# VectorE mixes the older block ahead of the last logits chunk of the newer one, in the second attention stage

## The chip, the cores and the metric

The kernel runs on one core of one Trainium2 chip. The metric is the device time of one execution in microseconds (us), inputs and output in the chip's memory.

## The reference, cut to what matters

The kernel computes a two-layer decoder trunk over 2048 tokens of width 1024. Layer 0 is a sparse attention, layer 1 a differential attention; each has its projections, a gate and an output projection. The change touches layer 1 alone:

```python
    def block(args):                      # one block of 128 queries, 8 heads, 2 maps each
        qb, start = args
        t = start + jnp.arange(BLOCK_Q)
        rel = t[:, None] - key_pos[None, :]
        bias = rel_bias[t5_bucket(rel)].astype(jnp.float32)
        logits = jnp.einsum('bqmd,blmd->bmql', qb, k).astype(jnp.float32)
        logits = logits + jnp.moveaxis(bias, -1, 0)[None]
        logits = jnp.where((rel >= 0)[None, None], logits, -jnp.inf)
        p = jax.nn.softmax(logits, axis=-1).reshape(bsz, B_HEADS, 2, BLOCK_Q, L)
        a = p[:, :, 0] - lam * p[:, :, 1]
        return jnp.einsum('bhql,blhe->bqhe', a.astype(v.dtype), v)
```

So for each head and block of queries there are two softmax maps; the second, scaled, is subtracted from the first, and the difference multiplies the values.

## The kernel before, in words

Both attention stages are written by one function, `stage_attention`; the second one is called with two maps (`M == 2`) and 8 heads. Each engine has its own program, and all of them walk the same list of places: 16 places a head, one block of 128 queries each, in the order of `ORDER` (blocks 2, 3, 6, 7, 10, 11, 14, 15, 12, 13, 8, 9, 4, 5, 0, 1 at places 0 to 15). Block b has (b + 1) x 128 keys, cut into chunks of up to 512, so there are 1, 1, 2, 2, 3, 3, 4, 4, 4, 4, 3, 3, 2, 2, 1, 1 chunks at places 0 to 15. "(p, i)" below is chunk i at place p, always both maps.

- **TensorE** (`logits`, `turn`, `values` in its program). A pair of logits chunks goes to two of four buffers in PSUM (`s_ps`, `SR = 4`), so the pair (p, i) may be written when VectorE has read the pair two before it. At place p TensorE issues (p, 1), (p, 2), (p, 3), each with one quad (up to 4 transposes) of the mixed block of place p - 3 beside it, then (p + 1, 0), then matmuls with the values. The transposes go to two PSUM buffers (`t_ps`, `TR = 2`) that ScalarE empties: the third quad waits for ScalarE's copy of the first.
- **VectorE** (`logits`, `invert`, `maximum`, `mix`). It copies each chunk out of PSUM to SBUF with bias and a running maximum (lines 1255, 1257), combines the maxima (line 1263), inverts the sum of the second map of the block before (line 1267, it waits for both exponentials of that block), makes the factor -lambda l1 / l2 (line 1273), and adds the scaled second map to the first (line 1275, the mix).
- **ScalarE** (`exps`, `leave`, `output`). At place p it computes both exponentials of the block of place p - 1 in place, with their sums (line 1321, waits for the maximum), then copies the transposes of the block of place p - 3 to SBUF (line 1329), then an output block (line 1338).

Each engine executes in its written order. `walk` writes places 0 to 5 of the first head, then a loop whose pass is places 6 to 15 of one head and 0 to 5 of the next, then the rest; so VectorE's loop jumps back between places 5 and 6.

## Time and profile before

| | us |
|---|---|
| median of 3 runs | 3835.47 |
| lowest, highest | 3829.93, 3839.96 |
| the profiled execution | 3832.36 |
| its span | 3830.6 |
| VectorE's part of the second attention stage | about 2784 to 3547 |

The profile shows one execution. "Busy" of an engine counts its instructions; an idle time carries the name of what ended it. TensorE's matmuls (PE) and weight loads (PEld) are counted apart. PEclk is TensorE's granted clock as a share of 2.4 GHz. In a timeline a row can stand for several instructions in a row (x4). Loads and matmuls wait separately, so one wait can be seen twice.

### The profile page before, as it was taken

To read this page: it belongs to the slowest core of one execution; us is meant where nothing else is said; L and a number is where in the kernel's file an instruction comes from. 1 tells how busy PE (TensorE), PEld (TensorE's weight loads), DVE (VectorE), ACT (ScalarE), POOL (GpSimd) and SP (SyncE) were. 2 spreads that over 40 slices of the span, in tenths; PEclk is the share of its full clock that TensorE was granted. 3 is DMA by queue.
4 is the path that set the end of the run, shared out by engine and by line. 5 is a ranking of instruction groups with operands and counts; after the bars stand their busy time and mean duration, and the time that the engine had idled before them with its cause. 6 is when DMAs were issued, how large, how long until landed. Compare 5 with 4: busy or idle time off the path is not lost. (4 is left out here: it accounts for less than half of the span.)

```text
span 3830.6 us, 65352 instructions
## 1 busy us (share of the span) xinstructions
PE 3446.8 (90%) x18786; PEld 2574.8 (67%) x18786; DVE 2133.8 (56%) x5870; ACT 2015.2 (53%) x3490; POOL 523.1 (14%) x550
## 2 busy tenths in 40 slices
PE   5869898888999999998966999999989988989799
PEld 3746454476666666666855888889966666666687
DVE  3659999995555555555643111000087777777343
ACT  3548799946777777774223111111066666666222
POOL 2000255001111111110211111111020000000011
PEclk7989999978999999998987999999989999999798
DMA  9651689573223322324532444222142222221442
GB/s 236 184 135 33 201 236 237 172 228 102 76 79 82 84 75 76 85 73 164 173 138 83 120 121 118 87 71 69 58 130 70 70 70 70 70 70 31 138 143 99
DMA packets 430048, 436.43 MB, mean 114 GB/s; under 512 B 81793, under 2 KB 341281, under 8 KB 429601
## 3 DMA queue, kind: packets, MB, share of 16 engines
q1 hardware_dynamic: 419072, 430.93, 38.6%
q10 hardware_dynamic: 10784, 3.18, 0.9%
q8 instruction: 92, 1.51, 0.2%
q14 instruction: 100, 0.81, 0.1%
HBM read 271.44 MB, written 162.53 MB: 113 GB/s over the span
## 5 line engine op out<-in xcount | busy, mean ns | idle before, releaser
L1255 DVE CUSTOM_DVE_ANT_0 a_att_sb_lg<-a_att_ps_s,mask 128x512 f32<-128x512 f32 (+3 forms) x512 | 302.2, 595 | 217.7 <-PE a_att_ps_s L1147 176.8
L1329 ACT ACTIVATE a_att_sb_pT<-a_att_ps_t 128x512 f32<-128x512 f32 (+3 forms) x640 | 315.9, 530 | 104.9 <-PE a_att_ps_t L1166 98.0
L1321 ACT ACTIVATE b_att_sb_lg<-b_att_sb_lg,b_att_sb_negm 128x384 f32<-128x384 f32 (+15 forms) x256 | 305.6, 1198 | 123.2 <-DVE b_att_sb_negm L1263 123.0
L1153 PE MATMUL b_att_ps_s<-b_att_sb_k,b_att_sb_q 64*128 64x512 f32 (+3 forms) x1920 | 297.1, 420 | 75.2 <-DVE b_att_sb_lg L1257 59.8
L1321 ACT ACTIVATE a_att_sb_lg<-a_att_sb_lg,a_att_sb_negm 128x384 f32<-128x384 f32 (+15 forms) x256 | 307.3, 1201 | 78.3 <-DVE a_att_sb_negm L1263 78.3
L1166 PE MATMUL a_att_ps_t<-ident,a_att_sb_lg 128*128 128x128 f32 x2176 | 340.0, 279 | 0.0
L1257 DVE TENSOR_SCALAR_CACHE_REDUCE b_att_sb_lg<-b_att_ps_s 128x512 f32<-128x512 f32 (+3 forms) x512 | 283.1, 590 | 90.1 <-PE b_att_ps_s L1153 75.0
L1694 DVE TENSOR_SCALAR_CACHE_REDUCE mask<-scores,threshold_bits 128x384 bf16<-128x384 f32 (+8 forms) x288 | 322.6, 1187 | 1.2
L1166 PEld LDWEIGHTS a_att_ps_t<-ident,a_att_sb_lg 128*128 128x128 f32 x2176 | 248.8, 141 | 107.3 <-issue 57.3
L1146 PE MATMUL a_att_ps_s<-a_att_sb_k,a_att_sb_q 128*128 128x512 f32 (+3 forms) x640 | 287.2, 449 | 26.5 <-DVE a_att_sb_mx L1255 15.7
L1183 PE MATMUL a_att_ps_o<-a_att_sb_pT,a_att_sb_v 128*64 128x256 f32 (+1 forms) x2304 | 297.4, 377 | 0.5 <-DMA a_att_sb_v<-scratch_v 0.5
L1664 ACT ACTIVATE mask<-scores,threshold_bits 128x1152 bf16<-128x1152 f32 (+4 forms) x160 | 274.6, 1717 | 22.4 <-DVE threshold_bits L1711 16.2
L1153 PEld LDWEIGHTS b_att_ps_s<-b_att_sb_k,b_att_sb_q 64*128 64x128 f32 x1920 | 164.8, 200 | 158.0 <-DVE b_att_sb_lg L1257 84.8
L1186 PE MATMUL b_att_ps_o<-b_att_sb_pT,b_att_sb_v 128*128 128x256 f32 (+1 forms) x1152 | 270.9, 384 | 0.0
L1610 PE MATMUL select_ps_acc<-select_sb_h,select_sb_w_gate 128*128 128x512 f32 x512 | 237.5, 619 | 29.6 <-DMA select_sb_w_gate<-in_a_w_in 20.7
L1186 PEld LDWEIGHTS b_att_ps_o<-b_att_sb_pT,b_att_sb_v 128*128 128x128 f32 x1152 | 214.7, 194 | 59.9 <-issue 18.2
L1114 POOL TENSOR_TENSOR a_att_sb_near_mask<-a_att_sb_near,mask 128x256 f32<-128x256 f32 x224 | 147.7, 671 | 729.6 <-DVE a_att_sb_mx L1255 377.1
L1329 ACT ACTIVATE b_att_sb_pT<-b_att_ps_t 128x512 f32<-128x512 f32 (+2 forms) x320 | 159.1, 527 | 158.6 <-PE b_att_ps_t L1166 157.7
L1147 PE MATMUL a_att_ps_s<-a_att_sb_k,a_att_sb_q 128*128 128x512 f32 (+3 forms) x640 | 235.2, 367 | 0.0
L1183 PEld LDWEIGHTS a_att_ps_o<-a_att_sb_pT,a_att_sb_v 128*64 128x64 f32 x2304 | 149.0, 136 | 120.9 <-issue 55.6
L405 DVE SCALAR_TENSOR_TENSOR b_qkgv_sb_o_lo<-b_qkgv_ps_acc,b_qkgv_sb_o_hi 128x512 f32<-128x512 f32 x64 | 44.2, 691 | 317.8 <-ACT b_qkgv_sb_o_hi L391 317.8
L391 ACT ACTIVATE b_qkgv_sb_o_hi<-b_qkgv_ps_acc 128x512 fp32r<-128x512 f32 x64 | 38.3, 599 | 324.3 <-PE b_qkgv_ps_acc L376 324.3
(282 smaller groups left out, 6941.7 us busy)
## 6 DMA issues: line engine op xcount, KB each, us to landing
a_att_sb_q<-scratch_qT SPq DMA_DIRECT2D x512, 64.0 KB, 2.6
select_sb_w_gate<-in_a_w_in SPq DMA_DIRECT2D x32, 512.0 KB, 5.6
mask_sb_mod_w<-in_mod_w SPq DMA_DIRECT2D x16, 1024.0 KB, 6.6
a_att_sb_k<-scratch_kT SPq DMA_DIRECT2D x128, 128.0 KB, 2.9
b_qkgv_sb_w<-in_b_w_in SPq DMA_DIRECT2D x32, 512.0 KB, 4.9
b_att_sb_q<-scratch_qT SPq DMA_DIRECT2D x128, 128.0 KB, 2.5
b_att_sb_k<-scratch_kT SPq DMA_DIRECT2D x64, 256.0 KB, 4.1
front_sb_mod_w<-in_mod_w SPq DMA_DIRECT2D x8, 1024.0 KB, 6.4
```

What stands on the lines that cost most here:

```text
L1146: nc.tensor.matmul(out, q[:, p // 2 % QS, 0, cols], k[:, slot, a:z], start=True, stop=False)
L1153: mm = nc.tensor.matmul(s_ps[:, (n + m) % SR, 0:z - a], q[rows, p // 2 % QS, x, cols], k[rows, slot, y, a:z], start=(j == 0), stop=(j == 2))
L1166: x = nc.tensor.transpose(t_ps[:, n % TR, j - a], lg[:, p % LR, j * P:(j + 1) * P], ident[:])
L1183: x = nc.tensor.matmul(o_ps[half, r % 2, a:PAIR], v[:, slot, j], pT[:, r % 2, j, a:PAIR], start=(j < 2 and not j == last == 1), stop=(j >= ...
L1186: x = nc.tensor.matmul(o_ps[:, r % 2, a:PAIR], v[:, slot, j], pT[:, r % 2, j, a:PAIR], start=(j == 0), stop=(j == last))
L1255: x = nc.vector.tensor_tensor_reduce(out, src, tab, 1.0, 2 * NEG, sign, ALU.max, top[:, col:col + 1])
L1257: x = nc.vector.tensor_scalar(out, src, 1.0, 2 * NEG, ALU.mult, ALU.max, accum_out=top[:, col:col + 1])
L1321: nc.scalar.activation(buf, buf, ACT.Exp, bias=negm[:, p, m:m + 1], accum_out=sums[:, b, ds(h * M + m, 1)]).then_inc(exp_done, 1)
L1329: nc.scalar.activation(pT[:, r % 2, a:z, c:c + P], t_ps[:, n % TR, 0:z - a], ACT.Copy).then_inc(t_left, 1)
L1610: m = nc.tensor.matmul(acc[:, t % RA], w_gate[:, j % 2, k], h[:, k], start=(k == 0), stop=(k == KD - 1))
L1664: nc.scalar.activation(junk[:, o:o + N], scores[:, o:o + N], ACT.Sign, bias=bits[:, place:place + 1].bitcast(F32), accum_out=cnt[:, place: ...
L1694: nc.vector.tensor_scalar(junk[:, o:o + N], scores[:, o:o + N], bits[:, place:place + 1].bitcast(F32), 0.0, ALU.is_ge, ALU.add, accum_out= ...
```

## The change

In VectorE's program `invert` and `mix` of the older block (place p - 1) are called together, ahead of the last chunk pair of the newer block (place p), and the maximum of the newer block comes behind that pair. Before, `invert` came behind the last chunk pair, then the maximum, and `mix` last. No instruction is added or taken away, and the programs of the other engines and the first attention stage (`M == 1`) stay as they are.

```diff
+            def mixing(h, p, before):
+                if M == 2:
+                    for head, x in both(h, p, before):
+                        if 1 <= x <= NB:
+                            invert(head, x - 1)
+                            mix(head, x - 1)
+
...
             def place(h, p, before):
                 if h is not None:
                     for i in range(NCH[p]):
+                        if i == NCH[p] - 1:
+                            mixing(h, p, before)
                         for m in range(M):
                             logits(h, p, i, m)
-                if M == 2:
-                    for head, x in both(h, p, before):
-                        if 1 <= x <= NB:
-                            invert(head, x - 1)
-                if h is not None:
                     maximum(h, p)
+                else:
+                    mixing(h, p, before)
                 for head, x in both(h, p, before):
                     for r in outputs_here(x):
                         output(head, r)
-                    if M == 2 and 1 <= x <= NB:
-                        mix(head, x - 1)
```

On VectorE, place 6 (block 14, four chunks) of the last head, before. `b_att_sb_lg` are the logits in SBUF, `b_att_ps_s` those in PSUM, `b_att_sb_mx` the maxima of the chunks, `b_att_sb_negm` the negated maximum; the mix of 1536 columns is that of block 11:

```order
L1257 TENSOR_SCALAR b_att_sb_lg,b_att_sb_mx<-b_att_ps_s 128x512 x6
L1257 TENSOR_SCALAR b_att_sb_lg,b_att_sb_mx<-b_att_ps_s 128x128
L1255 ISA b_att_sb_lg,b_att_sb_mx<-b_att_ps_s,b_att_sb_near 128x256
L1255 ISA b_att_sb_mx 128x1
L1257 TENSOR_SCALAR b_att_sb_lg,b_att_sb_mx<-b_att_ps_s 128x128
L1255 ISA b_att_sb_lg,b_att_sb_mx<-b_att_ps_s,b_att_sb_near 128x256
L1255 ISA b_att_sb_mx 128x1
L1267 RECIPROCAL b_att_sb_rec<-sums 128x1
L1263 TENSOR_REDUCE b_att_sb_negm<-b_att_sb_mx 128x2
L1273 SCALAR_TENSOR_TENSOR b_att_sb_ratio<-sums,b_att_sb_rec,neglam 128x1
L1275 SCALAR_TENSOR_TENSOR b_att_sb_lg<-b_att_sb_lg,b_att_sb_ratio 128x1536
```

And now:

```order
L1257 TENSOR_SCALAR b_att_sb_lg,b_att_sb_mx<-b_att_ps_s 128x512 x6
L1267 RECIPROCAL b_att_sb_rec<-sums 128x1
L1273 SCALAR_TENSOR_TENSOR b_att_sb_ratio<-sums,b_att_sb_rec,neglam 128x1
L1275 SCALAR_TENSOR_TENSOR b_att_sb_lg<-b_att_sb_lg,b_att_sb_ratio 128x1536
L1257 TENSOR_SCALAR b_att_sb_lg,b_att_sb_mx<-b_att_ps_s 128x128
L1255 ISA b_att_sb_lg,b_att_sb_mx<-b_att_ps_s,b_att_sb_near 128x256
L1255 ISA b_att_sb_mx 128x1
L1257 TENSOR_SCALAR b_att_sb_lg,b_att_sb_mx<-b_att_ps_s 128x128
L1255 ISA b_att_sb_lg,b_att_sb_mx<-b_att_ps_s,b_att_sb_near 128x256
L1255 ISA b_att_sb_mx 128x1
L1263 TENSOR_REDUCE b_att_sb_negm<-b_att_sb_mx 128x2
```

The inversion, the factor and the mix of block 11 moved from behind the last chunk pair of block 14 (two pieces of 128 and 256 columns a map) to ahead of it, and the maximum of block 14 closes the place.

On VectorE, the end of the loop's pass (place 5, block 11), before:

```order
L1261 REGISTER_ALU
L1262 REGISTER_ALU
L1263 TENSOR_REDUCE b_att_sb_negm<-b_att_sb_mx 128x2
L1272 REGISTER_ALU
L1273 ISA
L1273 SCALAR_TENSOR_TENSOR b_att_sb_ratio<-sums,b_att_sb_rec,neglam 128x1
L1274 REGISTER_ALU
L1275 SCALAR_TENSOR_TENSOR b_att_sb_lg<-b_att_sb_lg,b_att_sb_ratio 128x1408
L992 REGISTER_ALU
L992 COMPARE_AND_BRANCH
```

And now:

```order
L1257 TENSOR_SCALAR b_att_sb_lg,b_att_sb_mx<-b_att_ps_s 128x256
L1255 ISA b_att_sb_lg,b_att_sb_mx<-b_att_ps_s,b_att_sb_near 128x256
L1255 ISA b_att_sb_mx 128x1
L1239 REGISTER_ALU
L1257 TENSOR_SCALAR b_att_sb_lg,b_att_sb_mx<-b_att_ps_s 128x256
L1255 ISA b_att_sb_lg,b_att_sb_mx<-b_att_ps_s,b_att_sb_near 128x256
L1255 ISA b_att_sb_mx 128x1
L1261 REGISTER_ALU
L1262 REGISTER_ALU
L1263 TENSOR_REDUCE b_att_sb_negm<-b_att_sb_mx 128x2
L992 REGISTER_ALU
L992 COMPARE_AND_BRANCH
```

The mix of block 10 (1408 columns) was the last operation ahead of the jump; now the last chunk pair of block 11 and its maximum are.

## Rows read from the trace of the kernel before

**Rows 1.** The page, part 1: busy time, share of the span and instructions.
```profile
PE 3446.8 (90%) x18786; PEld 2574.8 (67%) x18786; DVE 2133.8 (56%) x5870; ACT 2015.2 (53%) x3490; POOL 523.1 (14%) x550
```

**Rows 2.** Busy time in eight stretches, one for each head of the stage: the sum.
```profile
sum 746.00, PE 670.64 PEld 478.80 DVE 591.61 ACT 474.98 POOL 20.26; mean PE 83.83 PEld 59.85 DVE 73.95 ACT 59.37 POOL 2.53
```

**Rows 3.** Waits, 2700 to 3600 us: engine line <- releaser, total us, times, longest.
```profile
ACT b_att_sb_lg L1321 <- DVE b_att_sb_negm L1263: 123.0, 65, 7.4
...
DVE b_att_sb_lg L1257 <- PE b_att_ps_s L1153: 75.0, 48, 7.3
...
PE b_att_ps_s L1153 <- DVE b_att_sb_lg L1257: 59.8, 57, 5.8
...
DVE b_att_sb_rec L1267 <- ACT b_att_sb_lg L1321: 9.7, 9, 3.9
...
PE b_att_ps_t L1166 <- DVE b_att_sb_lg L1275: 6.7, 2, 3.6
```

**Rows 4.** VectorE in time, blocks 6 and 7: start us, us, engine, line, operation, [idle <-releaser].
```profile
3077.03 0.29 DVE L1257 TENSOR_SCALAR_CACHE_REDUCE b_att_sb_lg<-b_att_ps_s 128x128 f32<-128x128 f32 x1 [1.55 <-PE b_att_ps_s L1153]
...
3078.35 0.17 DVE L1263 TENSOR_REDUCE b_att_sb_negm<-b_att_sb_mx 128x2 f32<-128x16 f32 x1
...
3078.82 0.75 DVE L1275 SCALAR_TENSOR_TENSOR b_att_sb_lg<-b_att_sb_lg,b_att_sb_ratio 128x512 f32<-128x512 f32 x1
...
3079.49 0.68 DVE L1257 TENSOR_SCALAR_CACHE_REDUCE b_att_sb_lg<-b_att_ps_s 128x512 f32<-128x512 f32 x1
...
3080.71 0.42 DVE L1257 TENSOR_SCALAR_CACHE_REDUCE b_att_sb_lg<-b_att_ps_s 128x256 f32<-128x256 f32 x1
```

**Rows 5.** ScalarE in time, the two exponentials of block 6.
```profile
3078.65 1.05 ACT L1321 ACTIVATE b_att_sb_lg<-b_att_sb_lg,b_att_sb_negm 128x896 f32<-128x896 f32 x1 [1.95 <-DVE b_att_sb_negm L1263]
...
3080.62 0.19 ACT L1321 ACTIVATION_READ_ACCUMULATOR b_att_sb_lg<-b_att_sb_lg,b_att_sb_negm  x1
```

**Rows 6.** VectorE in time: end and start of a loop pass, and other such starts.
```profile
3093.75 1.69 DVE L1275 SCALAR_TENSOR_TENSOR b_att_sb_lg<-b_att_sb_lg,b_att_sb_ratio 128x1408 f32<-128x1408 f32 x1
...
3098.15 0.69 DVE L1257 TENSOR_SCALAR_CACHE_REDUCE b_att_sb_lg<-b_att_ps_s 128x512 f32<-128x512 f32 x1 [2.72 <-issue]
...
3387.11 0.69 DVE L1257 TENSOR_SCALAR_CACHE_REDUCE b_att_sb_lg<-b_att_ps_s 128x512 f32<-128x512 f32 x1 [3.83 <-issue]
```

**Rows 7.** VectorE in time, the maximum of block 14 and, a place later, its mix.
```profile
3008.60 0.17 DVE L1263 TENSOR_REDUCE b_att_sb_negm<-b_att_sb_mx 128x2 f32<-128x16 f32 x1
...
3016.85 2.22 DVE L1275 SCALAR_TENSOR_TENSOR b_att_sb_lg<-b_att_sb_lg,b_att_sb_ratio 128x1920 f32<-128x1920 f32 x1
```

**Rows 8.** ScalarE in time, block 14: two exponentials, then copies of transposes.
```profile
3008.89 1.90 ACT L1321 ACTIVATE b_att_sb_lg<-b_att_sb_lg,b_att_sb_negm 128x1920 f32<-128x1920 f32 x1 [3.65 <-DVE b_att_sb_negm L1263]
...
3012.58 0.18 ACT L1321 ACTIVATION_READ_ACCUMULATOR b_att_sb_lg<-b_att_sb_lg,b_att_sb_negm  x1
...
3012.67 1.06 ACT L1329 ACTIVATE b_att_sb_pT<-b_att_ps_t 128x512 f32<-128x512 f32 x2
```

**Rows 9.** TensorE in time, places 7 to 10.
```profile
3013.80 2.03 PE L1153 MATMUL b_att_ps_s<-b_att_sb_k,b_att_sb_q 64*128 64x512 f32 x12
...
3015.76 1.99 PE L1186 MATMUL b_att_ps_o<-b_att_sb_pT,b_att_sb_v 128*128 128x256 f32 x8
...
3018.12 0.96 PE L1153 MATMUL b_att_ps_s<-b_att_sb_k,b_att_sb_q 64*128 64x512 f32 x6
...
3036.27 0.96 PE L1153 MATMUL b_att_ps_s<-b_att_sb_k,b_att_sb_q 64*128 64x512 f32 x6
```

**Rows 10.** TensorE in time, place 6 of the next head.
```profile
3102.56 1.65 PE L1153 MATMUL b_att_ps_s<-b_att_sb_k,b_att_sb_q 64*128 64x512 f32 x6 [0.44 <-DVE b_att_sb_lg L1257]
...
3104.14 3.35 PE L1186 MATMUL b_att_ps_o<-b_att_sb_pT,b_att_sb_v 128*128 128x256 f32 x8
```

**Rows 11.** Stretches: us, busy of PE, PEld, DVE, ACT, POOL, then granted clock.
```profile
3099.50:3107.50 8.00, 7.55 (x27) 5.37 (x28) 7.10 (x24) 3.45 (x3) 0.00 (x0) 0.50 0.00 1
...
3108.00:3113.00 5.00, 4.97 (x34) 2.74 (x32) 3.57 (x13) 1.96 (x4) 0.00 (x0) 0.99 0.00 0
```


## The prediction

> **What bounds the kernel now.** I read the page first, then the second attention stage by head, its waits, and the timelines of the three engines side by side over one head. On the page TensorE is busy 90% of the span and VectorE 56% [rows 1]. In the eight stretches of the changed stage, 93.3 us a head, they are busy 83.8 and 74.0 us [rows 2]: TensorE has 9.4 us of idle time a head, and the list of waits puts 59.8 us of it in the stage down to VectorE's reads of the logits buffers, against 75.0 us in which VectorE waits for logits [rows 3]. So a head has two halves. At the small blocks (places 10 to 15, 0 and 1) TensorE runs without a gap and VectorE waits for it. From the last chunk of block 6 (place 2), where VectorE still waits 1.55 us [rows 4], to about block 13 (place 9) VectorE runs almost without a gap and TensorE waits for its reads. Two further lines say how the mix stands: TensorE's transposes waited for a mix twice in the stage, 6.7 us in all, and VectorE's inversion waited for the exponentials 9 times, 9.7 us [rows 3]. An earlier mix serves nobody who waits; what decides is whether the exponentials are ready for it.
>
> **The order that is new.** Work and counts stay. Ahead of its last chunk pair of place p, VectorE now waits for both exponentials of block p - 1. Queued behind that wait are the mix, the last chunk pair, and with it the release of a logits buffer (TensorE waits for that) and the maximum (ScalarE waits for that: 123.0 us in the stage already [rows 3]). Before, the time from the maximum of block p - 1 to its inversion held one mix and all chunk pairs of p; now it holds no mix and all pairs but one.
>
> **Term 1, the waits in places 2 to 5.** The maximum of block 6 starts at 3078.35 and the first exponential at 3078.65, 0.3 later; the second ends at 3080.62 + 0.19 = 3080.81, so the pair takes 2.16 us for 896 columns [rows 4, 5]. For block 14 it takes 3008.89 to 3012.76, 3.87 us for 1920 columns [rows 8]. The line through both is 1.67 ns a column: 1.5 us for 512 columns, 2.4 for 1024, 3.0 for 1408, 3.4 for 1664, 4.1 for 2048. A full chunk pair costs VectorE 3080.71 - 3079.49 = 1.22 us [rows 4]. The wait is then about 0.3 us + the exponentials - 1.22 x (chunks - 1) - 0.1: 1.2 us at place 3 (block 7, one pair against block 6), 0.2 at place 4, 0.8 at place 5, nothing at 6, then 0.5, 0.7 and 0.1 at places 7 to 9. At place 2 the mix of block 3 fits the present gap of 1.55 us and could give back up to 1.1 us, but places 0 and 1 have one chunk each, so there the whole exponential pair is waited for (1.2 and 1.5 us) and VectorE arrives later; carried through those places, the first chunk of block 7 is read where it is read now, 3079.5. I count nothing gained. The waits sum to 1.2 + 0.2 + 0.8 = 2.2 us, of which 0.2 fall into small gaps that VectorE has there now, so it is 2.0 us later at the end of place 5: 8 x 2.0 = 16 us.
>
> **Term 2, the jump of the loop.** VectorE stands still at the jump between places 5 and 6: 2.72 us in one of its six passes back, behind a mix of 1.69 us, and 3.83 in another [rows 6]. If what it waits for runs from the last operation's issue, the mix now covers none of it, and up to 1.7 us comes on top; if not, nothing. I take half, 0.8: 6 x 0.8 = 5 us. The Trainium skill (Advanced Engine Details and Errata, Control Flow Timing) gives a branch about 0.05 to 0.11 us; by that the jump would cost nothing in either order and this term would be 0. The measured 2.72 and 3.83 us are far from that, so I stay with the rows.
>
> **Term 3, the ring through blocks 14, 15, 12, 13.** Four-chunk places carry more than VectorE's own waits, because the maximum now comes a mix later, and TensorE's third quad waits for ScalarE's first copy, which stands behind the exponentials, and with it the last logits. I go from the maximum of block 14, called 0 (3008.60 before [rows 7]). Exponentials 0.3 to 4.2, first copies to 5.2 [rows 8], then the logits (7, 3) and (8, 0), 2.03 us as in the row at 3013.80, values 1.99, four transposes, and (8, 1) is ready at 10.5; in the trace it is issued at 3018.12, 9.5 after the maximum [rows 9]. VectorE, with the mix (2.22 and 0.5 for its helpers) inside place 7, would want it at 9.8: it waits 0.8. The maximum of block 15 falls at 8.4, its exponentials end at 12.8, the mix of 2048 columns is over at 16.2, the maximum of block 12 falls at 16.7. Exponentials to 20.4, transposes and logits (9, 3) and (10, 0) to 23.6, values and one quad to 26.0, (10, 1) ready at 27.0. The maximum of block 13 falls at 24.5, its exponentials end at 28.5, two copies and quads later TensorE issues (11, 0) at 30.1. Before, this was at 3036.27, 27.7 after the same maximum [rows 7, 9]: 2.4 more. And the maximum of block 14 itself is a mix later (2.4 with helpers). So 4.8 us a head reach TensorE's gapless half. From below: VectorE's waits alone, 0.5 + 0.7 + 0.1 = 1.3. The chain is strict queues with durations of the rows, so I take it, less 0.5 for small gaps in VectorE's places 6 and 7 that swallow delay: 4.3 x 8 = 34 us.
>
> **What is hidden.** From place 11 to 15 and 0 to 1 the new waits (0.4, 1.8, 0.8, 2.2, 1.0, 1.1, 1.5 us by the same formula) lie in VectorE's own waiting for TensorE. The transposes keep two places of distance. If TensorE were faster there, these waits would come out as well. SyncE's and GpSimd's queues have nothing moved.
>
> **Sum.** 16 + 5 + 34 = 55 us on the profiled execution's 3832.4 (its span is 3830.6): 3887. The median of three runs is 3.1 us above that execution and within its spread; I give 3888.
>
> **The rivals.**
> A (forecast): the three terms, 3888, chance 0.48.
> B: only VectorE's own waits count, since TensorE's slack absorbs the later maximum: 2.0 + 1.3 = 3.3 us a head, 26 us, 3861 on the median. For it: TensorE waits 9.4 us a head already, so a part of the ring's delay may land there. Against: the delay enters after block 13, where there is no gap. Chance 0.22.
> C: the clock falls as well. After the idle time at the loop's jump the granted clock was 0.50 of 2.4 GHz for 8.0 us and 0.99 right behind [rows 11]; in the slow stretch six logits matmuls took 1.65 us and eight value matmuls 3.35, against 0.96 and 1.99 [rows 9, 10]. More waits of 1 to 2.5 us in places 3 to 9 can bring such a spell into a chain that is now the bound: one more spell a head, of which 3 to 4 us come out, is 28 us: 3915. Chance 0.18. The Trainium skill (Perfetto Trace Analysis, Matmul Optimizations) says that the engine scales its power with use and that matmuls should come back to back; that speaks against this change too.
> D (the other side): the mix fills the time in which VectorE waits for the last chunk, and the next chunks are read sooner. Place: places 2, 12 and 13, above all the 1.55 us at block 6 [rows 4]. It decides if the exponentials of block 3 are done when the first chunk of block 6 is read. Price: up to 1.1 us a head, if the later places then have no wait, and as much again at the following places: 8 x 2 = 16 us, 3819. Against: the formula gives waits at 3, 4 and 5 in all cases. Chance 0.05.
> E: the move is swallowed, within 0.3% (11.5 us): 3838. Chance 0.07.
>
> **How the numbers follow.** A measurement of this kernel can tell about 0.3%. A, B and C are slower by more than that: 0.88; E is the same, 0.07; D faster, 0.05. The range leaves out D, E and the tail of C: from B less a few us, 3853, to C with the jump's full 1.7 us (5 us more) and a little, 3926.
>
> **What would show it.** The wait of VectorE's inversion (line 1267) for ScalarE must rise from 9.7 us to about 8 x 14 = 100 us, with over 60 counts: place 3, and four-chunk places 7 and 8 of every head. If it stays under 40, the formula is wrong. TensorE's waits for VectorE's reads should rise by about 30 us and more, and its transposes, or weight loads of them, should wait for ScalarE's copies in places 7 to 10 (term 3); if instead (11, 0) is issued under 28 us after the maximum of block 14, B holds. At the loop's jump, the distance from the maximum of block 11 to the next read tells term 2: 2.7 us if nothing is added, 4.4 if all. A granted clock of 0.50 in more stretches than those behind the loop's jump tells C. The stage from 2784 to 3547 us should take some 55 us more, and all other stages nothing. Wrong altogether would be a stage that is no longer: then VectorE was never the bound between blocks 6 and 13.

## The result, and the profile after

The changed kernel takes 3925.31 us (median of 5 runs, 3920.28 to 3937.01) against 3835.21 (median of 5) for the kernel before on the same chip: a ratio of 1.0245, interval 1.0232 to 1.0258, or 90 to 94 us more. The prediction had the sign and the stage right, at 3888, and was 37 us too low; its range ended at 3926, and the ratio applied to the 3835.47 that it started from gives 3929.

The page of the changed kernel, part 1, as [rows 1]: no engine has gained or lost an instruction. The span grew from 3830.6 to 3927.0 us, by 96.4. TensorE is busy 42 us longer with the same 18786 matmuls, and idle the other 54.5.

```profile
PE 3488.7 (89%) x18786; PEld 2600.6 (66%) x18786; DVE 2144.9 (55%) x5870; ACT 2015.7 (51%) x3490; POOL 521.9 (13%) x550
```

The list of waits of the changed kernel, 2700 to 3750 us (engine line <- releaser: total us, times, longest). The exponentials are now at line 1325 and ScalarE's copies of transposes at line 1333:

```profile
ACT b_att_sb_lg L1325 <- DVE b_att_sb_negm L1263: 273.8, 101, 9.1
DVE b_att_sb_rec L1267 <- ACT b_att_sb_lg L1325: 110.3, 82, 3.2
...
DVE b_att_sb_lg L1257 <- PE b_att_ps_s L1153: 71.3, 51, 7.3
...
PE b_att_ps_s L1153 <- DVE b_att_sb_mx L1255: 46.5, 41, 2.7
...
PE b_att_ps_s L1153 <- DVE b_att_sb_lg L1257: 40.2, 49, 4.9
PE b_att_ps_t L1166 <- ACT b_att_sb_pT L1333: 39.2, 37, 2.4
...
DVE b_att_sb_lg L1257 <- issue: 22.6, 6, 4.9
```

and three lines of the same list of the kernel before, to go with [rows 3]:

```profile
DVE b_att_sb_lg L1257 <- issue: 10.5, 4, 3.8
...
PE b_att_ps_t L1166 <- ACT b_att_sb_pT L1329: 4.0, 16, 0.3
...
PE b_att_ps_s L1153 <- DVE b_att_sb_mx L1255: 3.7, 8, 0.5
```

Against [rows 3], the exponentials wait for maxima 273.8 us instead of 123.0, the inversion for exponentials 110.3 instead of 9.7, and TensorE's transposes for ScalarE's copies 39.2 instead of 4.0. TensorE's logits wait for VectorE's reads 86.7 us (46.5 + 40.2) instead of 63.5 (59.8 + 3.7); the prediction had said 30 or more on top. The maxima of the stage span 2784 to 3542 us before and 2785 to 3641 after: the whole loss lies in this stage, and begins with it.

From one start of block 11's maximum to the next is one head. The mean over the seven such distances, worked out from the starts of line 1263, is 96.3 us before (94.3 to 98.1) and 108.7 after (105.3 to 110.3), so 12.4 us a head. Three points split the six of them that hold a jump of the loop (heads 1 to 6, counted from 0). In the last column the predicted excess follows from the terms and the mixes that change sides of a point:

| a head with a jump, us | before | after | more | forecast |
|---|---|---|---|---|
| maximum of block 11 to that of block 14 (loop jump, place 6) | 10.36 | 12.86 | 2.50 | 0.6 |
| maximum of block 14 to (11, 0) issued (places 7 to 10) | 28.61 | 33.28 | 4.67 | 2.4 |
| (11, 0) to the next maximum of block 11 (the rest) | 57.03 | 63.18 | 6.15 | 3.9 |

The three come to 13.3 more; the forecast for all was 6.9. The middle row is 27.7 to 30.1 us before and 32.7 to 34.3 after, so the 27.7 from which the prediction started is the shortest of the six.

**The jump.** VectorE of the changed kernel, the end of a pass (start us, us, engine, line, operation, [idle <- releaser]), as [rows 6]:

```profile
3131.42 0.16 DVE L1267 RECIPROCAL b_att_sb_rec<-sums 128x1 f32 x1 [0.52 <-ACT b_att_sb_lg L1325]
...
3131.99 1.68 DVE L1275 SCALAR_TENSOR_TENSOR b_att_sb_lg<-b_att_sb_lg,b_att_sb_ratio 128x1408 f32<-128x1408 f32 x1
...
3135.17 0.17 DVE L1263 TENSOR_REDUCE b_att_sb_negm<-b_att_sb_mx 128x2 f32<-128x16 f32 x1
3140.04 0.69 DVE L1257 TENSOR_SCALAR_CACHE_REDUCE b_att_sb_lg<-b_att_ps_s 128x512 f32<-128x512 f32 x1 [4.70 <-issue]
```

The mix of block 10 (1.68 us) now stands ahead of the maximum, and behind the maximum VectorE stands still for 4.70 us. From the start of block 11's maximum to the next read it is 4.59 us in the mean of the six jumps (3.6 to 5.0), and 4.55 before (3.7 to 6.0), when a mix lay inside. The distance has not grown; the mix that used to lie in it now adds its own time ahead of the maximum.

**The chain.** VectorE of the changed kernel, the maxima of blocks 14, 15, 12 and 13 (places 6 to 9) and two waits between them, as [rows 7]:

```profile
3148.31 0.17 DVE L1263 TENSOR_REDUCE b_att_sb_negm<-b_att_sb_mx 128x2 f32<-128x16 f32 x1 [0.50 <-DVE b_att_sb_mx L1255]
...
3152.62 0.16 DVE L1267 RECIPROCAL b_att_sb_rec<-sums 128x1 f32 x1 [0.34 <-ACT b_att_sb_lg L1325]
...
3157.11 0.17 DVE L1263 TENSOR_REDUCE b_att_sb_negm<-b_att_sb_mx 128x2 f32<-128x16 f32 x1
...
3161.32 0.69 DVE L1257 TENSOR_SCALAR_CACHE_REDUCE b_att_sb_lg<-b_att_ps_s 128x512 f32<-128x512 f32 x1 [2.69 <-PE b_att_ps_s L1153]
...
3167.63 0.17 DVE L1263 TENSOR_REDUCE b_att_sb_negm<-b_att_sb_mx 128x2 f32<-128x16 f32 x1
...
3174.74 0.17 DVE L1263 TENSOR_REDUCE b_att_sb_negm<-b_att_sb_mx 128x2 f32<-128x16 f32 x1
```

ScalarE there, as [rows 8]: the exponentials of block 14, and behind them the copies for which TensorE waits.

```profile
3148.60 1.90 ACT L1325 ACTIVATE b_att_sb_lg<-b_att_sb_lg,b_att_sb_negm 128x1920 f32<-128x1920 f32 x1 [8.94 <-DVE b_att_sb_negm L1263]
...
3152.38 1.06 ACT L1333 ACTIVATE b_att_sb_pT<-b_att_ps_t 128x512 f32<-128x512 f32 x2
```

TensorE there, as [rows 9]:

```profile
3153.01 0.90 PE L1166 MATMUL b_att_ps_t<-ident,b_att_sb_lg 128*128 128x128 f32 x3 [2.15 <-ACT b_att_sb_pT L1333]
3153.84 2.93 PE L1153 MATMUL b_att_ps_s<-b_att_sb_k,b_att_sb_q 64*128 64x512 f32 x12
3156.69 3.25 PE L1186 MATMUL b_att_ps_o<-b_att_sb_pT,b_att_sb_v 128*128 128x256 f32 x8
...
3160.31 0.97 PE L1153 MATMUL b_att_ps_s<-b_att_sb_k,b_att_sb_q 64*128 64x512 f32 x6
...
3171.90 0.66 PE L1166 MATMUL b_att_ps_t<-ident,b_att_sb_lg 128*128 128x128 f32 x4 [1.72 <-ACT b_att_sb_pT L1333]
...
3181.24 0.96 PE L1153 MATMUL b_att_ps_s<-b_att_sb_k,b_att_sb_q 64*128 64x512 f32 x6
```

Everything is there that term 3 named. The transposes wait 2.15 us for a copy that stands behind the exponentials; the logits (8, 1), issued at 3160.31, are what VectorE waits 2.69 us for (0.8 forecast); two places on the transposes wait again, 1.72 us. What term 3 did not have is in the two rows behind the wait: twelve logits matmuls take 2.93 us and eight value matmuls 3.25, where the kernel before took 2.03 and 1.99 [rows 9].

The clock, in stretches of the changed kernel (us, busy of PE, PEld, DVE, ACT, POOL, then granted clock), as [rows 11]:

```profile
3124.00:3132.00 8.00, 7.02 (x33) 4.20 (x31) 6.79 (x27) 4.96 (x9) 0.00 (x0) 0.57 0.00 0
...
3135.00:3145.00 10.00, 5.64 (x24) 3.57 (x26) 4.48 (x18) 4.19 (x6) 0.00 (x0) 0.52 0.25 64
3145.00:3152.00 7.00, 5.54 (x34) 3.55 (x30) 6.45 (x21) 3.40 (x3) 0.00 (x0) 0.96 0.00 1
3152.00:3158.00 6.00, 5.00 (x18) 3.44 (x19) 5.20 (x17) 2.79 (x7) 0.00 (x0) 0.54 0.14 41
...
3172.00:3176.00 4.00, 4.00 (x20) 2.56 (x21) 3.25 (x8) 2.66 (x5) 0.00 (x0) 0.62 0.24 73
```

Before, a head had such a stretch around the jump, and in some heads short ones elsewhere. In this head there are now four: at places 4 and 5, around the jump, and behind each of the two waits of the transposes. Worked out from stretches of 2 us over heads 1 to 5, TensorE is at its lower level (1.2 of 2.4 GHz) for 8.9 us a head before and 25.3 us after.

### The profile page after: what moved, and what is told of

It is laid out like the page before. It is cut to its first block and busy times, and to the rows that moved or that the text cites. A ratio compares the mean times of both kernels' runs of the same rounds, so it can differ in the third digit from the quotient of the medians.

```text
span 3927.0 us, 65352 instructions
## 1 busy us (share of the span) xinstructions
PE 3488.7 (89%) x18786; PEld 2600.6 (66%) x18786; DVE 2144.9 (55%) x5870; ACT 2015.7 (51%) x3490; POOL 521.9 (13%) x550
## 5 line engine op out<-in xcount | busy, mean ns | idle before, releaser
L1325 ACT ACTIVATE b_att_sb_lg<-b_att_sb_lg,b_att_sb_negm 128x384 f32<-128x384 f32 (+15 forms) x256 | 305.7, 1197 | 274.0 <-DVE b_att_sb_negm L1263 273.8
L1153 PE MATMUL b_att_ps_s<-b_att_sb_k,b_att_sb_q 64*128 64x512 f32 (+3 forms) x1920 | 317.7, 447 | 98.5 <-DVE b_att_sb_mx L1255 46.5
L1146 PE MATMUL a_att_ps_s<-a_att_sb_k,a_att_sb_q 128*128 128x512 f32 (+3 forms) x640 | 287.1, 449 | 26.4 <-DVE a_att_sb_mx L1255 15.9
L1153 PEld LDWEIGHTS b_att_ps_s<-b_att_sb_k,b_att_sb_q 64*128 64x128 f32 x1920 | 178.3, 216 | 187.5 <-DVE b_att_sb_lg L1257 66.6
L1186 PE MATMUL b_att_ps_o<-b_att_sb_pT,b_att_sb_v 128*128 128x256 f32 (+1 forms) x1152 | 280.0, 393 | 0.0
L1166 PE MATMUL b_att_ps_t<-ident,b_att_sb_lg 128*128 128x128 f32 x1088 | 183.7, 296 | 45.4 <-ACT b_att_sb_pT L1333 39.2
```

Source lines behind the costliest of these rows:

```text
L1146: nc.tensor.matmul(out, q[:, p // 2 % QS, 0, cols], k[:, slot, a:z], start=True, stop=False)
L1153: mm = nc.tensor.matmul(s_ps[:, (n + m) % SR, 0:z - a], q[rows, p // 2 % QS, x, cols], k[rows, slot, y, a:z], start=(j == 0), stop=(j == 2))
L1166: x = nc.tensor.transpose(t_ps[:, n % TR, j - a], lg[:, p % LR, j * P:(j + 1) * P], ident[:])
L1186: x = nc.tensor.matmul(o_ps[:, r % 2, a:PAIR], v[:, slot, j], pT[:, r % 2, j, a:PAIR], start=(j == 0), stop=(j == last))
L1325: nc.scalar.activation(buf, buf, ACT.Exp, bias=negm[:, p, m:m + 1], accum_out=sums[:, b, ds(h * M + m, 1)]).then_inc(exp_done, 1)
```

## The experiments

All were run beside the kernel before on the same chip; a ratio is to that kernel and has its 95% interval. Most of them put the new order at some places only, which is one line beside the code of both orders:

```diff
+            EARLY_PLACES = range(2, 10)
...
+                early = h is not None and p in EARLY_PLACES
...
-                        if i == NCH[p] - 1:
+                        if early and i == NCH[p] - 1:
                             mixing(h, p, before)
```

At all other places invert, maximum and mix stand as before.

### Where in a head

`e_dve_half` has the new order at places 2 to 9, the half that VectorE bounds.

> The new order at places 2 to 9 only (blocks 6 to 13, the half in which VectorE sets the pace), the old one elsewhere. Theory R (the loss arises where VectorE and the ring of logits buffers set the pace: 12.5 us a head in the trace of the changed kernel): 80 to 95 us above before, nearly all of the change's 90. Rival S (the waits at the small blocks, 1 to 3 us each, are what costs, since they are the longest): 10 to 30 us above before.

3912.59 us, 1.0207 (1.0182 to 1.0231): 79 to 80 us, at the lower end of what was expected.

`e_pe_half` has it at places 10 to 15, 0 and 1.

> The complement: the new order at places 10 to 15, 0 and 1 only (blocks 8, 9, 4, 5, 0, 1, 2, 3), where TensorE runs without a gap. Theory R: within 10 us of before, though the inversions wait some 60 us for the exponentials there. Rival S: 60 us or more above before.

3840.48 us, 1.0026 (1.0013 to 1.0038): 8 to 10 us, although VectorE's inversion waits 87.5 us for exponentials in it, nearly as much as in the full change. The waits that a list puts at the top are mostly those that cost least: there VectorE would have waited for TensorE anyway. TensorE issues (2, 1) 39.9 us after (11, 0) in the kernel before, in this one and in the changed one. But "hidden" was not quite true, and less so in the full change: by the ratios the changed kernel is 15 us above `e_dve_half`. There the new order at place 2 meets exponentials of block 3 that are late: the maximum of block 6 comes 44.0 us after (11, 0), and 42.1 before, 42.3 in `e_pe_half` and 42.1 in `e_place2` below.

`e_jump_only` has it at place 5 (`EARLY_PLACES = (5,)`), ahead of the loop's jump.

> The new order at place 5 alone, the one ahead of the loop's jump. In both traces the next read comes 4.6 us (mean of six) after the start of the maximum of block 11, whether a mix of 1.7 us stands between or not. So if the jump's idle time is merely no longer covered: 6 x 1.9 = 11 us above before, and up to 5 more for the later maximum; 10 to 17 us. If the jump costs nothing of its own: within 4 us of before.

3847.09 us, 1.0035 (1.0022 to 1.0047): 13 to 15 us. The waits of the inversion stay at 9.7 us, none of them at place 5, and the standstill at the jump becomes that of the full change, in this row of its list of waits:

```profile
DVE b_att_sb_lg L1257 <- issue: 22.3, 6, 5.0
```

`e_not_at_jump` is its counterpart, all places but 5.

> The new order everywhere but at place 5. By the cover of the jump: 10 to 17 us below the changed kernel, 73 to 80 above before. If the jump has no part: the changed kernel's time, 88 to 92 above before.

3911.92 us, 1.0205 (1.019 to 1.022): 79 to 80 us, so place 5 gives 10 to 15 of the 90 to 94.

`e_place2` has it at place 2 alone (`EARLY_PLACES = (2,)`), where rival D saw a gain.

> The new order at place 2 alone (block 6), where VectorE stands 1.55 us before its last chunk and the exponentials of block 3 are done by then. Rival D of the prediction, kept to the one place where its condition holds: the first chunk of block 7 is read 1.1 us sooner, 8 x 1.1 = 9 us below before. If TensorE takes that back at once: the same as before within 3 us.

3825.66 us in five rounds, 0.998 (0.9971 to 0.9989): 6 to 8 us faster than before. VectorE of this kernel, block 6, to be read against [rows 4]:

```profile
3073.77 0.75 DVE L1275 SCALAR_TENSOR_TENSOR b_att_sb_lg<-b_att_sb_lg,b_att_sb_ratio 128x512 f32<-128x512 f32 x1
3074.80 0.29 DVE L1257 TENSOR_SCALAR_CACHE_REDUCE b_att_sb_lg<-b_att_ps_s 128x128 f32<-128x128 f32 x1 [0.27 <-PE b_att_ps_s L1153]
...
3076.12 0.17 DVE L1263 TENSOR_REDUCE b_att_sb_negm<-b_att_sb_mx 128x2 f32<-128x16 f32 x1
3076.33 0.69 DVE L1257 TENSOR_SCALAR_CACHE_REDUCE b_att_sb_lg<-b_att_ps_s 128x512 f32<-128x512 f32 x1
```

The mix fills the wait for the last chunk (1.55 us before, 0.27 now), and block 7's first chunk is read 0.21 us after the maximum of block 6 instead of 1.14 (3079.49 - 3078.35 [rows 4]). That is 0.9 us a head, 7 us in all, as measured. So D's mechanism was real at its place.

`e_blocks7_10` has the new order at places 3 and 4.

> The new order at places 3 and 4 only (blocks 7 and 10). Their blocks two and three places back have one or two quads, so no transpose waits for a copy behind the exponentials: only VectorE's own wait of 1.08 us at place 3 is left. Term 1: 8 to 12 us above before. Should the later maximum cost here as well: 20 us or more.

3846.03 us, 1.004 (1.0027 to 1.0053): 14 to 15 us, between the two outcomes. But it is not the wait of 1.08 us that it was to measure:

```profile
DVE b_att_sb_rec L1267 <- ACT b_att_sb_lg L1333: 10.8, 16, 3.9
```

The inversion waits 10.8 us in all, against 9.7 before, and at place 3 only 0.16 us a head. With the old order at place 2 the mix of block 3 still stands behind the maximum of block 6 and covers the rest. So what these 15 us pay for is the later maximum, not the wait.

`e_blocks15_12_13` has it at places 7, 8 and 9: term 3 by itself.

> The new order at places 7, 8 and 9 only (blocks 15, 12 and 13, four chunks each). VectorE's own waits for the exponentials sum there to under 1 us a head in the changed kernel's trace. Theory of term 3 (maximum a mix later, then exponentials, copies, third quad and next logits in a chain that reaches TensorE's gapless half): 30 to 50 us above before. Rival B (only VectorE's own waits count): 4 to 8 us above before.

3890.43 us, 1.0161 (1.0141 to 1.018): 59 us by the medians, 62 by the ratio, above the 30 to 50 expected. Three places out of sixteen make about two thirds of the loss, and the inversion's waits hardly count among them:

```profile
PEld b_att_ps_t L1166 <- ACT b_att_sb_pT L1341: 58.9, 64, 2.8
...
PE b_att_ps_t L1166 <- ACT b_att_sb_pT L1341: 38.4, 33, 2.4
...
DVE b_att_sb_rec L1267 <- ACT b_att_sb_lg L1333: 17.7, 23, 3.9
```

This is its list of waits: the inversion waits 17.7 us (9.7 before), the transposes 38.4 us for ScalarE's copies (4.0 before), and the logits 65.8 us for VectorE's reads (63.5 before), so the delay reaches TensorE through the copies and not through the logits buffers. Rival B, with VectorE's own waits alone, is out. The page of this kernel, part 1, shows how the loss divides on TensorE:

```profile
PE 3467.4 (89%) x18786; PEld 2586.4 (67%) x18786; DVE 2135.4 (55%) x5870; ACT 2017.4 (52%) x3490; POOL 522.8 (13%) x550
```

Its span is 3883.0 us, 52.4 more than before; 20.6 of them are longer busy time with the same matmuls, 31.8 are idle time.

By the ratios the parts come to 62 (places 7 to 9) + 13 (place 5) + 15 (places 3 and 4) - 8 (place 2) = 82, and `e_dve_half` gave 79; with the 10 of the other half, 92, against 94 for the whole. So the parts come to about the whole, within their intervals. That is a sum of runs and not of mechanisms: place 6 was never run alone, and the inversion's waits of 1.08 us at place 3 and 0.58 at place 5, which the changed kernel and `e_dve_half` have, are in none of the small runs.

### The wait or the late maximum

`e_invert_only` moves the inversion ahead of the last chunk pair, with its wait, and leaves the mix behind the maximum.

```diff
                         if i == NCH[p] - 1:
-                            mixing(h, p, before)
+                            inversion()
...
+                    if M == 2 and 1 <= x <= NB:
+                        mix(head, x - 1)
```

> Only the inversion, which carries the wait for the exponentials, goes ahead of the last chunk pair; factor and mix stay behind the maximum as before. Theory M (the cost is that a whole mix stands between the maximum of the older block and its exponentials' reader no longer, and ahead of the maximum of the newer one): the mix of p - 2 is back between the maximum and the inversion, so in blocks 6 to 13 the wait nearly vanishes and the time is within 15 us of before. Rival W (any wait for the exponentials ahead of the last chunk costs it in full, wherever the mix stands): 50 us or more above before.

3840.9 us, 1.0024 (1.0012 to 1.0036): 8 to 9 us with 54.8 us of inversion waits. But these waits stand at the small blocks, where VectorE waits for TensorE anyway: at places 2 to 9 they come to 0.16 us a head (heads 1 to 6), as its expectation said they would nearly vanish, against 2.5 in the changed kernel.

`e_lag2` does the reverse. Ahead of the last chunk pair it inverts and mixes the block of two places back, whose exponentials are long done, so the maximum comes as late as in the change but without the wait. It needs four buffers for the second map, and one weight piece of the output stage less is loaded ahead.

```diff
-EARLY_OUT = 5
+EARLY_OUT = 4
...
-LR, LR2 = 4, 2
+LR, LR2 = 4, 4
...
-                        if 1 <= x <= NB:
-                            invert(head, x - 1)
-                            mix(head, x - 1)
+                        if 2 <= x <= NB + 1:
+                            invert(head, x - 2)
+                            mix(head, x - 2)
```

> The mix stays ahead of the last chunk pair, but it is that of the block two places back (four buffers for the second map instead of two, paid by preloading four instead of five pieces of the output weights), so the exponentials are long done: the wait is away, the late maximum and the uncovered jump of the loop stay. If the wait for the exponentials is the main cause: 10 to 25 us above before, of which 11 for the jump. If the late maximum is (exponentials, copies, third quad, next logits in a chain): 45 us or more above before.

3887.39 us, 1.0128 (1.0097 to 1.0159): 49 to 55 us. In its list of waits the inversion's are gone, those of the transposes are there in full:

```profile
PEld b_att_ps_t L1166 <- ACT b_att_sb_pT L1333: 72.7, 65, 2.8
...
PE b_att_ps_t L1166 <- ACT b_att_sb_pT L1333: 48.1, 39, 2.4
...
DVE b_att_sb_rec L1267 <- ACT b_att_sb_lg L1325: 4.2, 2, 3.7
```

So the late maximum without the wait costs about 52 us, the uncovered jump among them, more than half of the loss. The other 38 to 45 us of the full change come only where the maximum is late and the inversion waits too. By the traces they lie between (11, 0) and the next maximum of block 11: 59.7 us in `e_lag2`, 63.2 in the changed kernel. No run has these waits without the late maximum: `e_invert_only` loses both. That the mix ahead of the maximum makes most of the loss is shown; how large the wait's part is by itself is not.

### The clock

`e_fill` is the changed kernel with idle transposes on TensorE (their result is not used) ahead of seven of its long waits in a head, 54 a head.

```diff
+            FILL = {(4, 1): (8, 0), (4, 2): (3, 0), (5, 1): (3, 0), (6, 1): (8, 0), (6, 2): (16, 0), (4, 2, 't'): (8, 1), (6, 2, 't'): (8, 2)}
...
+                    for _ in range(n):
+                        nc.tensor.transpose(o_ps[:, r % 2, 256:384], ident[:], ident[:])
```

> The changed kernel with idle transposes of the identity on TensorE (into free columns of an output bank) ahead of seven of its long waits in places 4 to 9, 54 a head, about 8 us at the full clock, no other change. Theory C (the low clock in spells behind those waits, 24 to 30 us a head against 8 to 10 before, is 2 to 4 us a head of the loss): the spells go, 20 to 35 us below the changed kernel. Rival (the spells cost nothing, as TensorE has slack there): the same time or some 10 us more, for the added work.

3913.7 us, 1.0215 (1.0201 to 1.023): 11.5 us below the changed kernel, where 20 to 35 were expected. In its trace the time at the lower clock fell from 25.3 to 6.1 us a head, less than the kernel before has. The three rows of the table, heads 1 to 6, are 11.8, 31.0 and 62.9 us: the first two fell by 1.1 and 2.3, and the middle one is now 2.4 above before, as forecast; the last has hardly moved. A head is 105.7 us long in the mean of these six, still 9.7 more than before. So the clock is a part of the loss, and not its main part.

`e_blocks_fill` puts 12 idle transposes ahead of two of TensorE's waits into the kernel with the new order at places 7 to 9.

```diff
+            FILL = {(4, 2, 't'): (12, 1), (6, 2, 't'): (12, 2)}
```

> The new order at places 7 to 9 alone (mixes of blocks 15, 12 and 13 ahead of the last chunk), which was 59 to 62 us slower than before, plus 12 idle transposes of TensorE ahead of two of its long waits for copies of ScalarE there (at places 7 and 9). In that kernel the granted clock was 0.50 for 17.8 us a head against 8.9 before. If the half clock is what puts the 62 above the 34 that the third term forecast: 40 to 44 us above the kernel before. If the chain itself is longer than I worked out: 60 us or more.

3878.75 us, 1.0111 (1.0094 to 1.0127): 43 to 46 us above before, where the same kernel without them had 59 to 62. That is near the 40 to 44 expected if the half clock is the excess. But the profiled executions of the two took 3884.6 and 3884.8 us and had 15.2 and 17.9 us a head at the lower clock, so the traces don't show where the 13 to 19 us of the medians went.

### ScalarE's order

If the loss runs from a late maximum through the exponentials to the copies behind them, ScalarE's order should matter. `e_copies_first` has the new order at places 7 to 9, and ScalarE makes its first two copies ahead of the exponentials at places 7 to 10.

```diff
+                first = 2 if M == 2 and p in (7, 8, 9, 10) else 0
+                for i in range(first):
+                    leave(back, t, i)
...
-                for i in range(4):
+                for i in range(first, 4):
```

> The new order at places 7 to 9 alone, plus ScalarE's first two copies of transposes placed ahead of the exponentials at places 7 to 10. If the chain maximum, exponentials, copies, third quad, next logits is what costs the 62 us, the transposes no longer stand behind a late maximum and most of it goes: at most 25 us above the kernel before. If the cost is VectorE's own (its reads and maxima late, whoever waits): still 55 to 65 us above.

3891.89 us, 1.0144 (1.0127 to 1.0161): 55 to 59 us, the second outcome. The waits of the transposes were gone all the same (4.0 us), but ScalarE now waited for the second quad before it could start the exponentials, and VectorE's inversion waited 71.8 us instead of 17.7. The edit brought a cost of its own, so the run tells nothing without controls. Those are the same moves with VectorE's old order: `e_copies_only` (two copies first) and `e_copy_only` (one), and between them `e_copy_first` (one copy first, new order at places 7 to 9).

> The order of before on VectorE, with ScalarE's first two copies of transposes ahead of the exponentials at places 7 to 10. It is the control of e_copies_first (59 us above before). If the moved copies cost by themselves, since the second copy waits for a quad of TensorE and holds the exponentials back: 25 to 45 us above before, and the new order on top of them costs 15 to 35. If they cost nothing: within 5, and then the chain through the copies isn't what the new order pays for.

> The new order at places 7 to 9 alone (59 to 62 above before), with the first copy alone ahead of the exponentials at places 7 to 10. The third quad waits for this copy only, and the copy's own quad is done early. If the chain exponentials, first copy, third quad, logits is the cause: 15 to 40 us above before. If not: 55 or more.

> The order of before on VectorE, with the first copy alone ahead of the exponentials at places 7 to 10; the control of e_copy_first. Expected within 10 us of before, since the third quad hardly waits for copies there (4.0 us in the stage), so that the difference of the two is the price of the new order without the chain.

| copies ahead of the exponentials | old order | new order at 7 to 9 | price of the new order |
|---|---|---|---|
| none | 1 | 1.0161 | 0.0161 |
| one | 1.0111 (1.0087 to 1.0134) | 1.0147 (1.0122 to 1.0172) | 0.0036 |
| two | 1.0041 (1.0028 to 1.0055) | 1.0144 (1.0127 to 1.0161) | 0.0103 |

In microseconds the price is 62, 14 and 39; by the intervals the 14 may be off by 13 either way and the 39 by 8. I had expected `e_copy_only` within 10 us of before; it is 41 to 43 above, and `e_copies_only`, expected at 25 to 45, is 15 to 16. So neither pair separates the chain cleanly. In the pair with two copies first the transposes wait 4.0 us for copies in both kernels, as before, and the new order still costs 39 us, with the inversion's waits at 71.8 against 40.3 us: there the same edit costs by another way than the copies. `e_copy_only` shows late exponentials by themselves, since VectorE's program in it is that of before. ScalarE of this kernel, place 10:

```profile
3150.56 0.60 ACT L1341 ACTIVATE b_att_sb_pT<-b_att_ps_t 128x512 f32<-128x512 f32 x1 [2.49 <-PE b_att_ps_t L1166]
3151.05 1.78 ACT L1333 ACTIVATE b_att_sb_lg<-b_att_sb_lg,b_att_sb_negm 128x1792 f32<-128x1792 f32 x1
...
3154.60 1.07 ACT L1341 ACTIVATE b_att_sb_pT<-b_att_ps_t 128x512 f32<-128x512 f32 x2
```

and TensorE there:

```profile
3155.23 0.66 PE L1166 MATMUL b_att_ps_t<-ident,b_att_sb_lg 128*128 128x128 f32 x4 [2.16 <-ACT b_att_sb_pT L1341]
3155.82 0.96 PE L1153 MATMUL b_att_ps_s<-b_att_sb_k,b_att_sb_q 64*128 64x512 f32 x6
3156.71 5.16 PE L1186 MATMUL b_att_ps_o<-b_att_sb_pT,b_att_sb_v 128*128 128x256 f32 x16
```

The maximum of block 13 is there at 3146.73, and the two places up to it take what they take before (7.05 and 7.21 us for blocks 12 and 13). The exponentials start at 3151.05, 4.0 us later than 0.3 behind the maximum, because a copy holds them. The transposes then wait 2.16 us for the next copy, (11, 0) is issued 32.35 us after the maximum of block 14 (3123.47) where it was 27.7 to 30.1 before, and the sixteen value matmuls behind it take 5.16 us, against 3.51 in the kernel before. So exponentials that are late for another reason than VectorE's order reach TensorE through the copies as well, and the matmuls behind the wait are slower again.

### A version that beats both

`v_two_heads` keeps what gained, the new order at place 2, and lets VectorE's loop pass over two heads, so that it jumps back twice in the stage and not six times.

```diff
+                with engine.Fori(0, heads // 2 - 1) as i:
+                    for u in range(2):
+                        for p in range(TAIL, NB):
+                            place(i * 2 + u, p, None)
+                        for p in range(TAIL):
+                            place(i * 2 + (u + 1), p, i * 2 + u)
```

> The new order at place 2 alone, and VectorE's loop written over two heads, so that it jumps back twice and not six times in the second stage. By the rows of the jump (next read 4.6 us after the maximum with a jump, 2.0 without): 4 x 2.6 = 10 us below the kernel with place 2 alone, that is 15 to 20 below before. If TensorE's and ScalarE's own jumps set the pace there: no more than place 2 alone.

3807.31 us, 0.994 (0.9922 to 0.9958), the fastest of all. The page's part 1 and a line of its waits, against 10.5 us before:

```profile
PE 3441.7 (90%) x18786; PEld 2570.6 (68%) x18786; DVE 2131.3 (56%) x5870; ACT 2016.2 (53%) x3490; POOL 523.0 (14%) x550
...
DVE b_att_sb_lg L1257 <- issue: 1.5, 1, 1.5
```

Against `e_place2` the four jumps less are worth 15 us by the ratios, 18 by the medians, about 4 us each. From the maximum to the next read a pass without a jump saves about 2.5 us (2.07 for 4.55, both with a mix in between), which makes the 10 us expected. What gave the other 5 to 8 was not separated; the time at the lower clock fell too, from 11.6 to 6.8 us a head. `v_two_heads_fill` adds 16 idle transposes a head ahead of (6, 2).

> As the last, with 16 idle transposes (2.4 us at the full clock) on TensorE ahead of the logits (6, 2), where it stands for 3 to 5 us behind the jump and comes back at half the clock. If the spell costs: 3 to 10 us less than without. If the wait is not there in most heads any more: 5 to 15 us more, for the added work.

3811.28 us, 0.9953 (0.9936 to 0.9969): the time at the lower clock falls from 6.8 to 4.1 us a head and no time is gained. What the idle transposes cost by themselves was not measured.

## Why the prediction was wrong in size

**Order, stage, sign: right.** The inversion's waits were forecast at about 100 us with over 60 counts and are 110.3 with 82. The prediction's "8 x 14" is 112; its own waits sum to 12.3 us a head, 98 in all, and the places that it names would give 24 counts. Most of the waits lie at the small blocks; at places 7 to 9 they are 0.2, 0.2 and 0 us (0.5, 0.7 and 0.1 forecast). TensorE's transposes wait for copies at places 7 to 10. The loss lies in the stage.

**Terms 1 and 2: right in sum, partly by luck.** They forecast 16 + 5 = 21 us for places 2 to 5; places 3, 4 and 5 cost 15 + 13 and place 2 gives 8 back, which makes 20. In the changed kernel term 1's waits are 1.08, 0 and 0.6 us at places 3 to 5, close to the forecast (1.2, 0.2 and 0.8). But the small runs that make up the 20 have next to none of them: `e_blocks7_10` pays for a later maximum, to which term 1 gave no cost. "I count nothing gained" at place 2 holds only with the new order at the small blocks: alone, place 2 gained 0.9 us a head. Term 2 took "half, 0.8". The jump leaves all of the mix uncovered: 1.9 us with its helpers in six jumps is 11 us. `e_jump_only` shows 13 to 15, with no wait of the inversion at place 5; the rest is the later maximum, which its expectation put at up to 5 us. Both ends stood in the text (2.7 and 4.4 us of idle time), and the row of 3.83 us was there; half was a choice between two mechanisms, of which the runs chose the dearer. The branch figure of the Trainium skill (Advanced Engine Details and Errata, Control Flow Timing), 0.05 to 0.11 us, is not what a jump costs here: the trace has 4.59 us from the last maximum to the next read with a jump, and 0.3 without.

**Term 3: the chain right, its price not.** This is the step that failed. Forecast 34 us, measured 59 to 62 with places 7 to 9 alone. Step by step in the rows above, after the maximum of block 14: the maximum of block 15 at 8.8 (8.4 forecast), the end of its exponentials at 13.2 (12.8), (8, 1) issued at 12.0 (10.5), the maximum of block 12 at 19.3 (16.7), that of block 13 at 26.4 (24.5), (11, 0) at 32.9 (30.1). The first step that is off by more than 0.4 is (8, 1), the one with TensorE in it. The logits ahead of it took 2.93 us and the values 3.25, 2.2 us longer than the 2.03 and 1.99 I put in. I took the durations of [rows 9], from a place where the granted clock was full, for a place where the same chain makes TensorE wait 2.15 us; [rows 11] showed what follows an idle time. Rival C named this and gave it one spell a head and 28 us; it came together with A, not in place of it. With the fillers of `e_fill` the distance to (11, 0) was 31.0 us in the mean, 2.4 above before as forecast.

**What was called hidden: 0 forecast, 8 to 10 us measured** (`e_pe_half`), and 15 on top of the other half. The inversion's waits for blocks 5, 0 and 1 are 2.5, 1.6 and 3.1 us by the changed kernel's timeline, above the 2.2, 1.0 and 1.1 that I had reckoned with. They are hidden up to (2, 1). Then the text had block 7's first chunk read where it is read before; in the changed kernel it is read 1.0 us later after (11, 0).

**The sum.** 20 for places 2 to 5, about 60 for 7 to 9, 8 to 10 for the rest make the 90 to 94 measured; the prediction had 21, 34 and 0. How the excess of term 3, some 26 us, divides is not settled. Three things speak for the clock: the row durations; the 20.6 us of longer busy time in `e_blocks15_12_13`, beside 31.8 of idle time, which is close to the 34 forecast; and 13 to 19 us by the medians and ratios of `e_blocks_fill`. In the whole changed kernel it is the same: 54.5 us of idle time, where 55 were forecast in all, and 42 of longer busy time. But such an account does not say what a full clock would give back: the 54 idle transposes a head of `e_fill` gave 11.5 us by the ratios, their own price already taken off, and a head of it is 9.7 us longer than one of before with less time at the lower clock. And of the 13.3 us more a head, what the last row of the table has above its forecast, 2.2, is hardly from the clock, since with the fillers it is still 2.0. That the chain runs through ScalarE is shown by the waits of the transposes in four kernels and by `e_copy_only`; that it is the only way is not shown, and the pair with two copies first speaks against it.

## What to carry to other kernels

On an engine that executes in its written order, ask of every operation not when it could run but what stands behind it: here a mix that nobody waited for was put ahead of a maximum on which exponentials, copies, transposes and the next logits hang in turn. Follow such a chain with durations from rows that were taken in the state which the change creates; matmuls behind a wait of 2 us took about half as long again, and that was the first visible miss. And test a move place by place: the same edit gained 0.9 us a head where VectorE waited for a last chunk, and lost elsewhere. But look in the trace of each small run whether the wait that it is to price is still there: here it had gone with the neighbour's old order.

## What the runs showed of the hardware that I had not expected

- With VectorE's jump back it is 4.55 us from the last maximum to the next read with a 1.7 us mix behind the maximum, and 4.59 without one; in passes without a jump the distance is 2.0 and 0.3 us. Four jumps less were worth 15 to 18 us.
- The granted clock fell to 0.50 around waits of about 2 us (2.15 and 1.72 in the rows above), 25.3 us a head in all, though not at every one: in `e_blocks15_12_13` TensorE waited 2.14 us ahead of 3157.50 and kept its clock. Behind `e_copy_only`'s 2.16 us wait the value matmuls took 5.16 us where they took 3.51, without any wait in front, in the kernel before.
- Idle transposes ahead of the waits brought TensorE's mean granted clock from 0.927 to 0.945, above the 0.939 of the kernel before, and with that only 11.5 of 94 us.
